# Order of SyncE's weight loads at the start of the second block: the two compression weights moved ahead of the second projection tile

## What is computed

```python
h = rms_norm_2(x, norm1_g[l])
proj = h @ w_in[l] + b_in[l]
(qa, ka, va, fa, qb, kb, vb, qc, kc_, vc_, ksl, vsl, kwn, vwn, gc, gates) = jnp.split(proj, split_at, axis=-1)
...
# inside nsa_attention: blocks of 32 tokens, stride 16, flattened and put through a small MLP
kc = compress_blocks(k_cmp, cmp_pe, k_w1, k_w2)
vc = compress_blocks(v_cmp, cmp_pe, v_w1, v_w2)
```

## Time and profile before

| what | value |
|---|---|
| median of 3 runs | 1022.88 us (1022.46 to 1024.64) |
| the profiled execution: its own time | 1022.46 us |
| the profiled execution: its span | 1020.7 us |
| TensorE matmul busy | 970.5 us (95% of the span) |
| GpSimd busy | 379.8 us (37%) |
| ScalarE busy | 385.4 us (38%) |
| mean granted TensorE clock | 0.984 |
| DMA, mean over the span | 247 GB/s |

### The profile page before, as it was taken

How to read it: one execution, slowest core, us unless ns; L and a number is a source line. 1 busy time by engine, 2 the same in 40 slices (tenths; PEclk the granted TensorE clock), 3 DMA queues, 4 the chain that set the end, 5 groups by cost and what they waited for, 6 DMA issues and landing times.

```text
span 1020.7 us, 15195 instructions
## 1 busy us (share of the span) xinstructions
PE 970.5 (95%) x6112; PEld 710.2 (70%) x6120; DVE 496.2 (49%) x853; ACT 385.4 (38%) x617; POOL 379.8 (37%) x249
## 2 busy tenths in 40 slices
PE   7999999999999998998699999999999999999997
PEld 3887677777788543444243699777565789999996
DVE  1555358544244622313031603546675368777775
ACT  2542345445433321211011644444543254434342
POOL 0885747444783054553310499740002500000000
PEclk8999999999999999999799999999999999999999
DMA  9996955334469899999999888533224465454521
GB/s 378 363 408 253 374 174 157 88 99 124 144 207 428 355 390 402 419 421 409 408 400 421 305 323 255 154 101 102 84 83 144 165 268 199 172 205 164 205 82 41
DMA packets 49274, 252.08 MB, mean 247 GB/s; under 512 B 10432, under 2 KB 11072, under 8 KB 31424
## 3 DMA queue, kind: packets, MB, share of 16 engines
q1 hardware_dynamic: 42736, 248.10, 64.2%
q0 software_dynamic: 6480, 3.17, 1.1%
HBM read 294.22 MB, written 1.05 MB: 289 GB/s over the span
## 4 chain that ended last, share of the span: by engine, by line
PE 74%; DVE 7%; DMA 6%; issue 6%; ACT 3%; POOL 2%; SPq 0%; DVEq 0%; POOLq 0%; ACTq 0%
PE ps L878 32%; PE ps L1201 17%; PE ps L1339 3%; DMA big<-in_mod_dram 2%; DMA big<-in_pieces_dram 2%; PE ps L1415 2%; PE ps L774 2%; PE ps L1354 2%; PE ps L826 1%; PE ps L1366 1%; DMA tail<-in_experts_dram,xidx 1%; PE ps L1297 1%; PE ps L1430 1%; POOL sel L2284 1%; PE ps L1105 1%
## 5 line engine op out<-in xcount | busy, mean ns | idle before, releaser
L2254 POOL TENSOR_TENSOR wl<-ring,wh 128x1024 fp32r<-128x1024 f32 (+5 forms) x132 | 289.3, 2211 | 227.3 <-ACT wh L1752 225.7
L1752 ACT ACTIVATE wh<-ring 128x1024 fp32r<-128x1024 f32 (+5 forms) x148 | 143.3, 983 | 135.6 <-PE ps L878 100.5
L878 PE MATMUL ps<-wh,hTh 128*128 128x512 f32 (+3 forms) x384 | 151.9, 396 | 1.6 <-DVE wl L3078 1.3
L878 PE MATMUL ps<-wl,hTh 128*128 128x512 f32 (+3 forms) x384 | 147.6, 384 | 0.0
L878 PE MATMUL ps<-wh,hTl 128*128 128x512 f32 (+3 forms) x352 | 136.3, 387 | 0.0
L1201 PE MATMUL ps<-hTs,wsp 128*128 128x256 f32 x1056 | 128.7, 283 | 0.5 <-DVE wsp L2914 0.5
L1201 PEld LDWEIGHTS ps<-hTs,wsp 128*128 128x128 f32 x1056 | 128.1, 192 | 1.5 <-DVE wsp L2914 0.7
L2242 POOL TENSOR_TENSOR small<-small 128x2 f32<-128x2 f32 (+2 forms) x7 | 5.3, 759 | 272.4 <-DVE small L3227 192.4
L878 PEld LDWEIGHTS ps<-wh,hTh 128*128 128x128 f32 x384 | 72.6, 189 | 23.6 <-issue 8.7
L878 PEld LDWEIGHTS ps<-wl,hTh 128*128 128x128 f32 x384 | 72.7, 189 | 13.6
L878 PEld LDWEIGHTS ps<-wh,hTl 128*128 128x128 f32 x352 | 66.3, 188 | 13.1
(11 more groups left out here) (479 smaller groups left out, 1661.4 us busy)
## 6 DMA issues: line engine op xcount, KB each, us to landing
big<-in_pieces_dram SPq DMA_DIRECT2D x43, 2048.0 KB, 15.1
ring<-in_wa_dram SPq DMA_DIRECT2D x68, 512.0 KB, 4.2
big<-in_mod_dram SPq DMA_DIRECT2D x11, 2048.0 KB, 10.7
ring<-in_ffn_dram SPq DMA_DIRECT2D x11, 2048.0 KB, 9.0
ring<-in_wb_dram SPq DMA_DIRECT2D x40, 512.0 KB, 3.7
dring<-in_ffn_dram SPq DMA_DIRECT2D x11, 1024.0 KB, 4.9
ring<-in_wb_dram SPq DMA_DIRECT2D x12, 384.0 KB, 5.6
ring<-in_pieces_dram SPq DMA_DIRECT2D x2, 2048.0 KB, 14.2
```

The source lines that it names most:

```text
L878: mm = pe.matmul(out, x[i], y[j], start=(p, c, k) == (0, 0, 0), stop=(c, k) == (KD - 1, 2), skip_group_check=True)
L1752: nc.scalar.activation(quarter(name, q, "high"), quarter(name, q, "raw"), ACT.Copy).then_inc(s_qh, 1)
L2254: nc.gpsimd.tensor_tensor(quarter(name, q, "low"), quarter(name, q, "raw"), quarter(name, q, "high"), ALU.subtract).then_inc(s_ql, 1)
```

## The change

The loop over `LOADS2` does its extra work behind its first tile, fox, and all of it at once. SyncE now issues: the four quarters of fox, the wait for the last scatter, the two tables, ck, the two halves of cv, and only then the four quarters of dilq, and the rest as before without ck and cv between. No wait is added or taken away, and no load changes its size or place. The helper `compress_weights` goes; its loads are written into the loop.

```diff
-            def compress_weights(i, name, *parts):
-
-                at, size = offs[name]
-                for dst in parts:
-                    n = size // len(parts)
-                    sp.dma_start(dst, wb[:, at:at + n].rearrange("p (c n) -> p c n", n=CH)).then_inc(s_cw[i], 16)
-                    at += n
-
+            first = True
             for name, _, _ in LOADS2:
                 n = NL[name]
                 load_into(name, wb, n - n0 >= 2 and n - 2)
-                if name == "dilq":
+                if first:
                     sp.wait_ge(s_sca, NALL + 3)
                     sp.dma_start(cst[:, CONST1:], consts[:, CONST1:]).then_inc(s_table, 16)
                     sp.dma_start(bias2, rows[0:1, ROW["b2v"][0]:NROW].partition_broadcast(P)
                                  ).then_inc(s_table, 16)
-                elif name == "dilk":
-                    compress_weights(0, "ck", ckw)
-                elif name == "nsaq":
-                    compress_weights(1, "cv", *cvw)
+                    for i, name in enumerate(("ck", "cv")):
+                        at, size = offs[name]
+                        parts = ((ckw, size),) if i == 0 else ((cvw[0], size // 2), (cvw[1], size // 2))
+                        for dst, size in parts:
+                            sp.dma_start(dst, wb[:, at:at + size].rearrange("p (c n) -> p c n", n=CH)
+                                         ).then_inc(s_cw[i], 16)
+                            at += size
+                    first = False
```

## The result

The changed kernel took 1027.53 us (median of 7 executions, 1025.52 to 1036.07) against 1022.88 us (median of 7, 1022.46 to 1024.64). The ratio is 1.0051, with a 95% interval of 1.0031 to 1.0073: slower by about 5 us, as forecast (1027.9). With the 17 further executions on record, 24 in all, its median is 1028.31 us, 5.4 above the kernel before. The execution that was profiled took 1030.03 us, with a span of 1028.2 us.

The account below looks back on a forecast made before the run. TensorE was taken as the bound, with no wait left to end. A 3.45 us stall before dilq plus 1.6 us of lower clock gave 5.05 us, forecast 1027.9 us, 0.5% slower; range from 1025.1, a little lowered, to 1030.6.

Parts of the forecast that it names:

- The bound: TensorE holds 74% of the chain and is busy throughout 580 to 650 us, so no wait can be ended.
- Served in order: SyncE's queue serves loads in issue order, so dilq's first quarter lands only after 7.60 MB.
- Term 1, the stall: TensorE waits before dilq, starting it at 594.4 in place of 590.94: 3.45 us.
- the upper bound of 6.1: Longest stall before dilq, in us, with bytes at 396 GB/s and up to 2 us of tail.
- the tail of the slowest engine: dilq's landing waits for the slowest DMA engine, up to 2 us after the bulk of the bytes.
- Term 2, the clock: After the stall, about 3.4 us at 1.2 GHz in the midst of dilq, costing 1.6 us.
- the rival without a clock drop: The stall of 3.45 us before dilq comes but the clock stays up: 1026.3 us, chance 0.16.
- The slow queue: Slowest DMA engine's tail and 396 GB/s delay dilq: stall 6.1, clock 1.6, 1030.6 us, chance 0.13.
- The sum: Stall before dilq and clock drop together: 3.45 + 1.6 = 5.05 us.
- Given back: Sign that would refute the prediction: TensorE makes the lost time good before 646 us.
- The faster rival: nsaq and kcvw land sooner, ending ScalarE's wait for kcvw: at most 1.3 us gained, 1021.6 us, chance 0.03.
- The 358 GB/s of the Trainium skill: Limit on HBM loads per core, by which dilq's bytes take 21.2 us and the stall is 6.1 us.

Follow-up runs that it names:

- e1: Kernel before with ck and cv moved up behind the tables, dilq left in front of the wait for the scatter: 1022.89 us, ratio 0.9999.
- e2: Kernel before with only dilq moved, behind the wait for the scatter and the two tables: 1022.55 us, ratio 1.0002.
- e3: Kernel before with dilq behind the wait, the tables and ck, cv left behind nsaq: 1023.10 us, ratio 1.0002.
- e7: Kernel before with dilq behind the wait, tables, ck and first half of cv: 1022.70 us, timed again 1024.11 us.
- e6: Changed kernel with dilq's four loads issued on ScalarE's queue: 1025.30 us, ratio 1.0026.
- the second profile: The changed kernel timed and profiled again without an edit: 1028.51 us, ratio 1.0054.
- e5: Changed kernel with 16 matmuls on zeros on TensorE between fox and dilq: 1026.94 us, ratio 1.0036.
- e10: Changed kernel, all on SyncE's queue, with ck and cv in four loads each of 4096 byte rows: 1027.62 us, ratio 1.0049.

## Why the prediction was right

**The bound.** Right: TensorE's chain is the bound, and no wait was there to end. e1 and e2 show that each other part of the change is worth 0, as costed, within about 1 us.

**Served in order.** Right. The doses in e3, e7 and the changed kernel put the landing by the bytes in front, and a second queue (e6) moves it forward.

**Term 1, the stall: 3.45 us forecast, 5.0 and 5.1 measured in the profiles.** The mechanism held, the size was low, within the upper bound of 6.1. The step was the landing at 20.6 us after the tables' issue (2.15 + 18.5); it was 22.3. The bulk ran a little faster than the 410 GB/s that I took: 420 from 578 to 592. The start ran slower. From the issue to 578 I had 5.44 us at 410 GB/s, 2.23 MB; the window from 572 to 578 moved 6 x 0.329 = 1.97 MB. The little that moved from 570.4 to 572, 0.15 MB, was in part still fox, and is left out. The other 5.63 MB at 420 GB/s take 13.4 us and would be in at 591.4. The landing was at 592.75. The last 1.3 us are of the kind that the prediction had set aside as the tail of the slowest engine and kept for the upper bound. The packets from 572 to the landing bear it out:

```profile
DMA packets 1079, 8.16 MB, mean 393 GB/s; under 512 B 113, under 2 KB 113, under 8 KB 565
```

That is some 0.56 MB more than the 7.60 up to dilq's first quarter. At 420 GB/s it is the 1.3 us: some engines were already at the loads behind, while the last of them still had a share of this one. Which engine was last is not known. So -0.3 for the bulk, 0.6 for the start and 1.3 for the tail make the 1.7 us, up to rounding. Why the start ran at 329 GB/s was not tried.

**Term 2, the clock: 1.6 us forecast, 1.43 measured** in dilq's stretch, and a lower clock for twice as long in the second profile. e5 shows the cause: with the stall filled, the clock stays up. After stalls of 5 us the clock fell in all three profiles that had them (both of the changed kernel, and e10), after those of 1.4 to 2.5 us in none of the three of e7. The 2.6 us wait of the earlier trace rows, from which the prediction argued, did bring one. So a wait of that length among dense matmuls did not do what it does in the expert stage, as the rival without a clock drop had said; that rival was wrong for the 5 us of this kernel. No profile has a stall of the 3.45 us forecast, so whether the clock would have fallen at that length is not shown.

**The slow queue.** The landing, 22.3 us after the tables' issue, is nearer to this rival's 23.3 than to the 20.6 of the forecast. Its tail was there, its 396 GB/s for the bulk was not.

**The sum.** 5.05 us forecast, 4.65 between the medians, 5.4 with all 24 executions and 5.8 in the second timing, and 6.6 in the profiled stretch. So the mechanism was right and the closeness of the number is in part luck: the stall was 1.55 us longer than forecast, and the two terms as profiled are more than the medians show. That executions without the profiler stall a little less, or miss the clock drop in part, would explain it; it was not settled, since only profiled executions show the stall.

**Given back.** Nothing was: from the end of the lower clock, 598.6, to 645 TensorE is busy in 46.40 of 46.40 us.

**The faster rival.** Wrong, as its own objection said. In e1 ck and cv are early and dilq is in time, so its condition holds, and the ratio is 0.9999.

**The 358 GB/s of the Trainium skill** (DMA: Bandwidth & Descriptors, Where 436 GB/s comes from). The window after has 420 GB/s over 14 us, so this bound does not hold for this kernel on one core. The landing alone would hardly have told: by this estimate dilq lands 23.4 us after the tables' issue, and it was 22.3.

## What to carry to other kernels

Before a load is moved behind others in one queue, add up the bytes from the first issue to the load itself and divide by the rate that the trace shows in a full stretch; add a tail for the last engine (1.3 us here); compare with the time at which the first engine that touches the data, and not only the last, needs it. A load that is early by 15 us by its issue can be late by 5 by its landing. A stall of TensorE of some 5 us costs 1.4 us more than its length, through the clock, or twice that where the lower clock lasts twice as long.

## What was not expected of the hardware

**Two queues share by rows.** A load of short rows beside one of long rows gets a small share (92 of 423 GB/s for 3072 byte rows beside 8192), since each queue gets one row in turn; that equal rows would give equal shares follows from this, but was not run by itself. Its service also began late: in e6 no packet of dilq moved in the first 2.6 us behind its issue (579.4 to 582), and the first quarter took 8.7 us to land. Why it began late stays open.

**Two paces of the same matmuls.** The stretch without a stall took 57.83 us for 468 matmuls in the kernel before and in e2, and 59.62 us in e1, at a granted clock of 1.00 in both (chain: start, us, what; e2, then e1):

```profile
578.47 57.83 PE ps L882 x468
```

```profile
578.00 59.62 PE ps L880 x468
```

The matmuls start 0.113 us apart at the one pace and some 0.118 at the other. dilq to vv took 48.58 us in e7's first profile and in e5, and 47.22 in e7's other two, all at full clock, so the slower pace costs about 1.4 us in this stretch, as much as the clock drop. The pace can change within an execution: e5, e7's first profile, e10 and the second of the changed kernel have fox at the faster pace (73 matmuls in 8 us) and dilk at the slower one (138 or 139 in 16 us). All four have a stall in between. But the first profile of the changed kernel and two of e7 have a stall too and keep the faster pace, and e1 and e6 are slow from fox on, before any. So it is not shown that a stall brings the slower pace. If it does in part, that is a share of the cost of a stall that no term of the prediction has. What sets the pace stays open.
